# A ring of four PSUM banks for attention scores: jobs of up to 512 keys take one bank, wider ones two

## The reference, cut to what matters

```python
def block(args):                       # one block of 128 queries, all keys up to it
    s1 = einsum('bhqd,bhkd->bhqk', q1b, k1) * scale_d
    s2 = einsum('bhqd,bhkd->bhqk', q2b, k2) * scale_d
    p = softmax(where(chunk_mask, s1, NEG)) - lam * softmax(where(chunk_mask, s2, NEG))
    od = einsum('bhqk,bhkd->bhqd', p, dv_t)
    sf = einsum('bhqd,bhkd->bhqk', qfb, fk_t) * scale_f + cqb[..., None] - cum[:, :, None, :]
    of = einsum('bhqk,bhkd->bhqd', softmax(where(causal, sf, NEG)), fv_t)
...
def _stick_breaking(q, k, v):          # second layer, one block of 128 queries
    z = einsum("bhqd,bhkd->bhqk", qb, kb) * scale
    log_1m = where(mask, log_sigmoid(z) - z, 0.0)
    a = where(mask, exp(log_sigmoid(z) + reverse cumsum of log_1m), 0.0)
    out = einsum("bhqk,bhkd->bhqd", a, vb)
```

## Time and profile before

| what | value |
|---|---|
| median of 3 runs | 2509.6 us |
| profiled execution, its own time | 2510.65 us |
| its span, first to last instruction | 2508.9 us |
| TensorE busy | 2438.6 us, 97% |
| VectorE busy | 1709.4 us, 68% |
| ScalarE busy | 1029.8 us, 41% |
| GpSimd busy | 1058.8 us, 42% |
| mean granted TensorE clock | 0.991 |

### The profile page before, as it was taken

The page is one execution under the profiler, slowest core; times in us unless marked ns, Lnnn a source line. Parts: engine busy times, 40 slices in busy tenths (PEclk is TensorE's granted clock), DMA queues, the critical chain, the costliest instruction groups (busy, mean ns, idle before and its releaser), DMA issues.

```text
span 2508.9 us, 31192 instructions
## 1 busy us (share of the span) xinstructions
PE 2438.6 (97%) x11626; PEld 2000.6 (80%) x11626; DVE 1709.4 (68%) x2375; ACT 1029.8 (41%) x1733; POOL 1058.8 (42%) x717
## 2 busy tenths in 40 slices
PE   8999999999899999999999999999989999999998
PEld 6767788878688888888887877887878888888886
DVE  5676667673786766776778966777396566656663
ACT  5455555562532322222245536554252232323232
POOL 4666641211534444444454553431353343434344
PEclk9999999999999999999999999999999999999998
DMA  4312221132111111111113852222211111112121
GB/s 146 85 47 57 88 59 39 59 115 73 46 42 51 56 56 54 51 51 55 55 55 109 187 125 68 59 74 93 74 43 51 51 55 47 55 47 59 42 64 72
DMA packets 152373, 170.20 MB, mean 68 GB/s; under 512 B 10656, under 2 KB 108704, under 8 KB 152096
## 3 DMA queue, kind: packets, MB, share of 16 engines
q1 hardware_dynamic: 149056, 156.67, 20.6%
q0 software_dynamic: 3168, 11.54, 2.5%
HBM read 122.55 MB, written 15.20 MB: 55 GB/s over the span
## 4 chain that ended last, share of the span: by engine, by line
PE 83%; DVE 9%; ACT 3%; issue 2%; POOL 2%; DMA 1%; SPq 0%; DVEq 0%; ACTq 0%; POOLq 0%
PE PS L1590 23%; PE PS L1595 23%; PE PS L1592 23%; PE PS L1682 3%; PE PS L1669 2%; PE PS L1703 2%; PE PS L1700 2%; PE PS L1663 2%; DVE R L1987 1%; DVE R L2004 1%; DVE rstd L2000 1%; PE PS L1666 1%; DVE Pb L1879 1%; DVE sm L1865 1%; DVE Pb L1877 1%
## 5 line engine op out<-in xcount | busy, mean ns | idle before, releaser
L1590 PE MATMUL PS<-R,wh 128*128 128x512 f32 x2952 | 1169.7, 396 | 9.9 <-ACT R L2173 3.6
L1595 PE MATMUL PS<-R,wh 128*128 128x512 f32 x2952 | 1155.0, 391 | 13.1 <-DVE R L2004 12.9
L2377 POOL TENSOR_TENSOR lows<-values,wh 128x512 fp32r<-128x512 f32 (+1 forms) x409 | 601.9, 1475 | 1044.5 <-ACT wh L2150 940.8
L1592 PE MATMUL PS<-R,lows 128*128 128x512 f32 x2512 | 982.6, 391 | 0.5 <-POOL lows L2377 0.5
L1595 PEld LDWEIGHTS PS<-R,wh 128*128 128x128 f32 x2952 | 556.1, 188 | 135.2 <-DVE R L2004 15.9
L1590 PEld LDWEIGHTS PS<-R,wh 128*128 128x128 f32 x2952 | 557.2, 189 | 122.2 <-issue 3.8
L1592 PEld LDWEIGHTS PS<-R,lows 128*128 128x128 f32 x2512 | 474.3, 189 | 93.0 <-issue 3.4
L2150 ACT ACTIVATE wh<-values 128x512 fp32r<-128x512 f32 (+1 forms) x409 | 255.1, 625 | 704.3 <-PE PS L1595 676.7
L1991 DVE TENSOR_TENSOR X<-PS,X 128x512 f32<-128x512 f32 x400 | 272.0, 691 | 238.9 <-PE PS L1595 238.9
L2377 POOL TENSOR_TENSOR late_r<-late,wh 128x512 fp32r<-128x512 f32 x83 | 126.8, 1528 | 130.6 <-ACT wh L2150 96.2
L1968 DVE TENSOR_TENSOR stage<-PS,stage 128x512 f32<-128x512 f32 x154 | 104.6, 687 | 103.1 <-PE PS L1595 102.8
(11 more groups left out here) (268 smaller groups left out, 2805.6 us busy)
## 6 DMA issues: line engine op xcount, KB each, us to landing
values<-w_in_dram SPq DMA_DIRECT2D x92, 256.0 KB, 2.9
values<-w_ff_dram SPq DMA_DIRECT2D x92, 256.0 KB, 2.8
R<-R SPq DMA_DIRECT2D x96, 128.0 KB, 2.3
X<-X POOLq DMA_DIRECT2D x22, 512.0 KB, 6.1
values<-w_up_dram SPq DMA_DIRECT2D x40, 256.0 KB, 3.0
values<-w_gate_dram SPq DMA_DIRECT2D x38, 256.0 KB, 3.0
late<-w_ff_dram SPq DMA_DIRECT2D x36, 256.0 KB, 3.0
values<-w_down_dram SPq DMA_DIRECT2D x32, 256.0 KB, 2.7
```

The costliest lines, as they stand in the source:

```text
L1590: e.matmul(PS[:, b, :], wh, high, start=s["start"], stop=False)
L1592: e.matmul(PS[:, b, :], wl, high, start=False, stop=False)
L1595: m = e.matmul(PS[:, b, :], wh, low, start=False, stop=s["stop"])
L2377: e.tensor_tensor(T.wl[piece.v][:, 0:m], T.wv[piece.v][:, 0:m], T.wh[:, piece.h, 0:m].bitcast(F), ALU.subtract).then_inc(*sg.up("w_lo", pi ...
```

## The change

`score_banks(n)` takes the place of `SB`. It holds a pointer into a ring of four banks, 0 to 3. A narrow job takes the bank under the pointer alone; a wide one rounds up to an even bank and takes two. The claims, and the events left on the banks after the exp, go by the banks taken. Four narrow jobs can so hold scores at once; a wide job behind wide ones still shares the ring with one other. Since each unit has its narrow jobs in multiples of four, the rounding never skips a bank.

```diff
 class Attention:
-    SB, OB = [0, 2], 5
+    OB = 5
...
-        self.job = self.group = self.turned = 0
+        self.job = self.group = self.turned = self.bank = 0
...
+    def score_banks(self, n):
+
+        if n <= 512:
+            banks = [self.bank]
+        else:
+            self.bank = (self.bank + 1) // 2 * 2 % 4
+            banks = [self.bank, self.bank + 1]
+        self.bank = (self.bank + len(banks)) % 4
+        return banks
+
     def scores(self, u, a, i):
         O = self.O
         n = 128 * (i + 1)
-        s = self.SB[self.job % 2]
-        j = dict(u=u, a=a, i=i, n=n, s=s, slot=self.group % 2, no=self.job, key=(self.name, self.job), o=8 + 8 * (self.job % 6))
-        O.step("scores", j=j, given=O.claim(s) + O.claim(s + 1), mask=list(self.mask), bias=list(self.bias) if u.kind == FOX else [])
+        banks = self.score_banks(n)
+        s = banks[0]
+        j = dict(u=u, a=a, i=i, n=n, s=s, banks=banks, slot=self.group % 2, no=self.job, key=(self.name, self.job), o=8 + 8 * (self.job % 6))
+        O.step("scores", j=j, given=[event for b in banks for event in O.claim(b)], mask=list(self.mask), bias=list(self.bias) if u.kind == FOX else [])
...
-        O.bank_given[j["s"]] = [("exp", j["key"])]
-        O.bank_given[j["s"] + 1] = [("exp", j["key"])]
+        for b in j["banks"]:
+            O.bank_given[b] = [("exp", j["key"])]
```

## The result

The changed kernel takes 2514.16 us (median of 18 executions, 2510.67 to 2519.42), the kernel before 2509.66 in 18 beside it: ratio 1.0018, 95% interval 1.0012 to 1.0024. It is 4.5 us slower, where 2.5 us of gain were forecast; the time lies 0.16 us above the stated range. In a later set of runs it took 2514.55 (ratio 1.0016, 1.0006 to 1.0025). The profiled execution took 2514.43 us.

A forecast was written before the change was run, and what follows sets the result against it. TensorE was taken as the bound, so only its own gaps in attention could be won. The terms -2.0 - 2.0 + 1.5 = -2.5 us, from a median of 2509.6, gave 2507.0 us, range 2500 to 2514.

The forecast's parts named there:

- 2.0 us for this term: Attention: scores of narrow jobs, and wide ones behind narrow, stop waiting for banks; 2.0 us won, bounds 1.3 to 2.3.
- What the new order moves: a2 and c0: reordering removes three TensorE waits and a pair of table loads; 2.0 us won, lower bound nothing.
- What it adds: Transposes closer behind their scores wait for VectorE's normalisation, sized at a0's start; 1.5 us lost, bounds 0 and 8.
- they keep their condition: Attention: wide scores behind wide ones still wait for the job two before; 9.2 of 10.4 us of bank waits remain.
- The clock: Three clock falls in attention, no change counted; bounds 6.8 us won if all go, 1.7 us lost for one more.
- the large rival: Large gain: gaps of the moved units close and clock falls, as at 166.90, go with them; 2500 us, chance 0.23.
- no effect: Attention: transposes take over every wait that the scores gave up, so the terms cancel; 2509.6 us, chance 0.13.
- The slower one: a0 to a2, c0 to c2: TensorE spends dense work late, waits for VectorE before transposes; 2515.6 us, chance 0.22.
- The marks: Signs set beforehand: score waits at starts of a0, a3, c0 gone, transpose waits 5 or 6 us, 37 table loads.
- the slow side: Sign of a slower outcome: first three units' TensorE idle over 14 us, busy time unchanged, transposes the largest share.

The follow-up runs named there:

- e1: Ring of single banks at run time, but every engine's program in the order of the kernel before; 2509.67 us, ratio 0.9993 to the kernel before.
- e12: Ring everywhere, but the new order in a0 and a1 only, the rest in the order of before; 2508.60 us, ratio 1.0000 to the kernel before.
- e3: The change, banks and order, in the second layer's attention only; 2512.03 us, ratio 1.0007 to the kernel before.
- e13: Ring everywhere, the new order everywhere but in a2; 2512.25 us, ratio 1.0010 to the kernel before.
- e18: Ring everywhere, the new order in the first layer but not in a2 or the second layer; 2510.89 us, ratio 1.0001 to the kernel before.
- e2: The change, banks and order, in the first layer's attention only; 2513.36 us, ratio 1.0011 to the kernel before.
- e8: The changed kernel run again unedited, for a second profiled execution; 2514.55 us, ratio 1.0016 to the kernel before.
- e6: Ring everywhere, but the planner told of it only for b0 to b3; 2511.78 us, ratio 1.0012 to the kernel before.
- e7: The changed kernel without the planner's preference for scores (20 becomes 0); 2524.08 us, ratio 1.0059 to the kernel before.
- e17: The changed kernel, planner also preferring VectorE's evacuations of projected stages by 40 places; 2510.92 us, ratio 0.9999 to the kernel before.
- e10: The changed kernel with some scores issued again to fill long TensorE waits; 2513.42 us, ratio 1.0021 to the kernel before.

## Why the prediction was wrong, point by point

**"2.0 us for this term" (the bank waits that go).** Wrong in what it was taken for. The waits at 89.73, 287.39 and 1543.08 do go when only the banks are changed (e1), but a wait gone from TensorE's timeline isn't time gone. e1 is 0.7 us below before by the medians and 1.8 by the ratio, with an interval that holds both 2.0 and nothing, so its time can't judge the term. The starts of the triples can: of the three waits 0.2 us is left, the rest stands as new waits right behind the old ones. The lower bound of 1.3 should have been 0, the same "if each turns into another wait" that I allowed the next term.

**"What the new order moves", -2.0.** The waits named were partly won: 224.88 is gone, 219.96 is now 0.90 at 221.94, the pair of table loads and the wait at 1527.13 are gone, but a dense triple waits 0.79 for its stage at 1545.33. e12 holds the new order of a0 and a1 alone and gains nothing measurable; e3, with c0 to c2, isn't faster either. The lower bound, nothing, was right.

**"What it adds", +1.5: this is the step that failed.** It was sized from transposes at the start of a0, as if bunched scores could make only transposes late. They did hardly: L1693 waits about as long as before in the first layer. What came instead is a new wait of wide scores behind wide scores, 2.96 us at 233.39, in a2: I had listed the existing waits of this kind, written that "they keep their condition", and not asked where the new order would make another. Before, two rotations and VectorE's 1.8 us for their stage stood between job 43 and job 44; that wait covered the exps. Now jobs 42 to 45 follow each other, and the rotations come after. The new order of a2 costs about 2 us (e13 against the changed kernel, e18 against e2, the triples 86 to 212), and c0 to c2 about as much again, in c1 with 1.8 us more idle over 32 triples; the part of b0 to b3 is open. That the run of four wide jobs is what costs within a2 is read from its trace; no run undid it alone. The term for the order is at least the 4.5 us measured, by the ratios some 6, not 1.5 - 2.0.

**The clock** ("I count no change"). The places of the falls changed, the total in the profiled execution did not (20.5 us between 80 and 2480 us in both). The price set for a fall (half its length) was right in one place, near 233 us in the order of before (1.6 us for 3.4), and wrong in the new order near 165 and 233 us (0.1 and 0.3 us). The changed kernel's first trace has no fall at 165 us, as the large rival wanted, and the 1.7 us that the rival counts for it did not come: with a fall there (e8) the stretch takes 0.1 us more. The fall at 1501.50 was in no run filled.

**The rivals.** The large gain and no effect are refuted by the ratio's interval, though "no effect" is right for the ring without its order. The slower one had the right sign and a time 1.4 us off (2515.6), but not its place: waits before L1693 grew from 3.4 to 4.2 us, where it needed 9.

**The marks.** 37 table loads: right. The waits of scores at the starts of a3 and c0 are gone; at the start of a0 there are two others, 0.44 us at 90.02 and 0.28 at 93.49. The transposes wait 4.2 us, not 5 or 6. Waits at 543 to 548 and 1705 to 1712: there, within 0.3 us. "TensorE idle over 14 us in the first three units" was to mark the slow side; it is 12.6, since much of the loss lies behind them. a3, c3 and the feed-forward stretches are the same within 0.4 us, so the loss is where the order differs.

**What stays open.** Within a2 the moves of single instructions brought nothing back, which leaves the run of four wide jobs or something else in its order; how much of c's part is c1 was not separated by a run. e6 says that b alone costs about 3 us (1.0012), which is as direct as anything said of a2, and b0 has the new wait of 1.79 us at 348.49. e18 says that b costs next to nothing beside a0 and a1, and the triples 212 to 500 take less than 1 us more. The intervals of e6 and e18 overlap (1.0003 to 1.0010), and I can't decide between them.

## What to carry to other kernels

A freed buffer has two effects, the wait that it ends and the order that a planner makes of it. Run them apart (new buffers, old order) before believing a sum of both. For the order, don't only re-read the waits that exist: look in the new sequence for work of the same kind that now stands in a row, for what used to cover it, and for what was queued in between on the other engine. And don't add up closed gaps on a busy engine while another, here VectorE, hands out the next one.

## What the runs showed of the hardware

**A fall of the granted clock costs half its length in one place and next to nothing in another.** The clock fell to 0.50 for 3.4 us at a time, right behind idle time of TensorE (1.8 us near 233 in e1). In the order of before it cost 1.6 us there; in the new order 0.3 us there and 0.1 near 165, where the next wait became 1.0 us shorter. Falls also differ between executions of one kernel: the changed kernel has none near 165 and 233 us in its first trace and one at each in e8. The mean clock over the executions does not tell the time: 0.9925 at 2508.7 us (e1), 0.9910 at 2514.3 (the changed kernel) and 0.9880 at 2524.6 (e7), but 0.9899 at 2509.9 (e17) and 0.9928 at 2514.8 (e10), all means.

**One VectorE multiply of the same shape took 0.62 us and 1.55 us.** The TENSOR_SCALARs over 128x768 at 234.22 before and at 233.57 after are shown above. GpSimd in the changed kernel, just then:

```profile
233.40 1.30 POOL L2414 TENSOR_TENSOR stage_r<-stage,R 64x512 fp32r<-64x512 f32 x1
234.78 1.48 POOL L2388 TENSOR_TENSOR lows<-values,wh 128x512 fp32r<-128x512 f32 x1
```

In the kernel before GpSimd is idle from 234.07 to 234.78. The evacuations, which read PSUM, take 0.67 to 0.68 us in both. The Trainium skill ("SBUF — State Buffer", SBUF: two separate sides) says that VectorE and GpSimd share a pair of ports under an exclusive lock, held for the whole instruction. The trace agrees with it: 0.93 us more for the multiply that meets a GpSimd instruction. It holds beyond the pair: of the 12 multiplies of this shape in the kernel before (L1879), the six during which GpSimd was idle took 0.62 us each, and the five that it ran beside for 0.4 us or more took 0.81 to 1.55. So a new order also changes the price of what it moves, which no step of my sum had.
